# Compression rows streamed from whole pages over several queues, and routing in fewer, batched steps

## The reference

```python
def compress(raw, pe, w1, w2):
    n = S // CMP_BLOCK
    x = raw.reshape(B, n, CMP_BLOCK, 2, N_KV, HEAD_DIM) + jnp.transpose(pe, (1, 0, 2))[:, :, None, :]
    x = jnp.transpose(x, (0, 1, 3, 4, 2, 5)).reshape(B, n, 2, N_KV, CMP_BLOCK * HEAD_DIM)
    hdn = jax.nn.gelu(jnp.einsum('bnsgf,sfh->bnsgh', x, w1))
    return jnp.einsum('bnsgh,shd->bnsgd', hdn, w2)
```

## Time and profile before

| | us |
|---|---|
| median of 3 runs | 1498.45 |
| the three runs | 1494.69, 1498.45, 1502.95 |
| the profiled execution | 1498.93 |
| its span | 1496.8 |

### The profile page before, as it was taken

How to read it: one execution, slowest core, us unless ns; L and a number is a source line. 1 busy time by engine, 2 the same in 40 slices (tenths; PEclk the granted TensorE clock), 3 DMA queues, 4 the chain that set the end, 5 groups by cost and what they waited for, 6 DMA issues and landing times. The chain is left out here.

```text
span 1496.8 us, 21480 instructions
## 1 busy us (share of the span) xinstructions
PE 1282.4 (86%) x7890; PEld 929.3 (62%) x7891; DVE 742.0 (50%) x1547; ACT 528.9 (35%) x873; POOL 108.5 (7%) x159
## 2 busy tenths in 40 slices
PE   4289999999538989999997999279999999999962
PEld 1156666665326556656666887167788887788731
DVE  0012222221212545656676666768856658675248
ACT  0010000100000137755555221157646457665132
POOL 1000011000000000000000000001101001110040
PEclk9599999999757559999999999569999999999986
DMA  9753345500432063000003332559976769975572
GB/s 328 237 162 137 134 162 90 97 12 12 100 88 81 14 213 126 2 1 1 2 2 103 112 118 106 191 185 371 375 261 240 268 245 362 376 248 207 204 285 94
DMA packets 100626, 237.69 MB, mean 159 GB/s; under 512 B 19914, under 2 KB 27525, under 8 KB 100391
## 3 DMA queue, kind: packets, MB, share of 16 engines
q1 hardware_dynamic: 88951, 196.47, 39.3%
q0 software_dynamic: 8144, 27.62, 5.1%
q10 hardware_dynamic: 3456, 12.58, 2.1%
HBM read 198.61 MB, written 40.13 MB: 159 GB/s over the span
## 5 line engine op out<-in xcount | busy, mean ns | idle before, releaser
L2079 PE MATMUL psum<-w_hi,x_parts 128*128 128x512 f32 x736 | 240.3, 398 | 8.4 <-DVE x_parts L2198 7.5
L2191 DVE TENSOR_TENSOR w_lo<-raw,w_hi 128x2048 fp32r<-128x2048 f32 x96 | 215.6, 2288 | 56.8 <-ACT w_hi L2138 56.7
L2138 ACT CAST w_hi<-raw 128x2048 fp32r<-128x2048 f32 x96 | 178.5, 1912 | 93.5 <-DVE work L2209 50.6
L592 PE MATMUL psum<-low,high 128*128 128x512 f32 (+5 forms) x576 | 200.3, 502 | 0.0
L2079 PEld LDWEIGHTS psum<-w_hi,x_parts 128*128 128x128 f32 x736 | 139.9, 190 | 39.9 <-issue 11.0
L592 PEld LDWEIGHTS psum<-low,high 128*128 128x128 f32 (+1 forms) x576 | 105.4, 188 | 77.5 <-issue 66.9
L2079 PE MATMUL psum<-w_lo,x_parts 128*128 128x512 f32 x368 | 144.6, 393 | 0.0
L1501 DVE CUSTOM_DVE_ANT_0 low<-psum,high 128x512 f32<-128x512 f32 (+3 forms) x160 | 88.8, 593 | 78.1 <-PE psum L1341 77.8
L2079 PE MATMUL psum<-w_hi,a_parts 128*128 x368 | 121.2, 401 | 5.6 <-DVE a_parts L2204 5.5
L1469 ACT ACTIVATE low<-low,high 128x640 f32<-128x640 f32 (+7 forms) x128 | 93.0, 729 | 51.4 <-DVE high L1501 51.4
L1664 PE MATMUL psum<-wo_parts,mix_parts 128*128 128x512 f32 (+1 forms) x432 | 104.0, 398 | 6.8 <-DVE wo_parts L1801 6.2
(11 more groups left out here) (310 smaller groups left out, 1519.9 us busy)
## 6 DMA issues: line engine op xcount, KB each, us to landing
raw<-in_moe_w_gate SPq DMA_DIRECT2D x16, 2048.0 KB, 11.2
raw<-in_moe_w_up SPq DMA_DIRECT2D x16, 2048.0 KB, 12.0
raw<-in_moe_w_down SPq DMA_DIRECT2D x16, 2048.0 KB, 11.2
high<-in_w_mod SPq DMA_DIRECT2D x12, 2048.0 KB, 13.9
y_d<-work ACTq DMA_DIRECT2D x24, 512.0 KB, 7.0
high<-in_x_prompt SPq DMA_DIRECT2D x16, 512.0 KB, 3.9
y_d<-high SPq DMA_DIRECT2D x1, 8192.0 KB, 37.3
low<-in_w_in SPq DMA_DIRECT2D x3, 2048.0 KB, 15.1
```

Of the source, the lines that this page charges most:

```text
L592: mm = pe.matmul(c.bank(2 + n % 2)[0:T, 0:w], hT[i % 2][:, k, 0:T], c.w_in[:, k, a:a + w], start=(k == 0), stop=(k == KT - 1))
L2079: mm = pe.matmul(out, left[l][:, k * P:(k + 1) * P], w[:, bass.ds(at + k * step, 512)], start=n == 0, stop=n == len(steps) - 1)
L2138: act.copy(c.w_hi[:, at:at + PART // 2], c.raw[:, o:o + PART // 2]).then_inc(hi_done[p], 1)
L2191: dve.tensor_tensor(c.w_lo[:, at:at + PART // 2], c.raw[:, o:o + PART // 2], c.w_hi[:, at:at + PART // 2].bitcast(F32), ALU.subtract).then ...
```

## The change

In compression a piece becomes two whole rows: a partition holds a pair of rows as it lies in memory, 2 KB of it, so a prompt tile is one DMA and a page is one DMA into 64 partitions. There are eight buffers instead of three. SP asks for each sample's first page, GpSimd for its second; ScalarE asks for `w2` and `w1` at the block's start. Since the halves no longer land side by side, ScalarE copies each tile into one of two buffers `pairs`, in the order that the transposes want. `xcT` is written as [2][16][192], so that each product reads its 192 columns side by side.

In routing, independent steps lose their link; the constants come in two loads, the small one first; the count product comes first and alone, and the prefix over tiles is done by eight more products that add shifted counts in PSUM; the operands of these and of the slot products are 16-bit (0, 1, multiples of 128 and numbers under 128). The 36 comparisons become one over 594 elements, one over 2304, and two multiplications by 594; the token's number is carried in two parts, its row and its tile. The weights' sums move to the end of the block. Of `block_routing` only added lines are shown; those that they replace stand above.

```diff
@@ constants, memory_routing
-    cols = [strict, np.tile(NE - np.arange(NE), (P, 1)), np.tile(4 - np.arange(4), (P, 1)),
-            np.tile(MB * np.arange(1, 9), (P, 1)),
-            np.tile((np.arange(NE)[:, None] > np.arange(NE)[None, :]).reshape(1, -1), (P, 1)),
-            np.tile(np.arange(MAX_SLOTS + 1), (P, 1)), r[:, None] + P * np.arange(NT)[None, :], np.tile(r, (P, 1))]
+    cols = [np.tile(NE - np.arange(NE), (P, 1)), np.tile(4 - np.arange(4), (P, 1)),
+            np.tile(np.append(-1, MB * np.arange(1, 9)), (P, 1)), strict,
+            np.tile(MB * (np.arange(NE)[:, None] > np.arange(NE)[None, :]).reshape(1, -1), (P, 1)),
+            np.tile(r, (P, 1)), np.tile(P * np.arange(NT), (P, 1)), r[:, None]]
     c["cph4"] = np.concatenate(cols, 1)
     return {k: np.ascontiguousarray(v, np.float32) for k, v in c.items()}
...
-    c.scratch, = allocate(c, 0, ("scratch", 9216, F32))
+    c.scratch, c.scratch_16 = allocate(c, 0, ("scratch", 7168, F32), ("scratch_16", 4096, BF16))
...
@@ block_compression
-    xcT = c.view(W_, 4, NPAIR)
+    nblk = NC_P + NC_S * NB
+    xcT = c.view(W_, 2, CB // 2, 2 * nblk)
     w1 = c.view(W_ + 4 * NPAIR, 2, CB // 2, P)
     o = W_ + 4 * NPAIR + 2 * (CB // 2) * P
-    nat = [c.view(o + 512 * s, 4, 2, HD) for s in range(3)]
-    o += 3 * 512
+    NAT = 8
+    nat = [c.view(KVR_ + 1024 + 512 * s, 2, 4, HD) for s in range(NAT)]
...
+    def load_page(eng, n, pg):
+
+        if n >= NAT:
+            eng.wait_ge(paired, n - NAT + 1)
+        at = (n - 4) * NPAGE + pg
+        page = eng.value_load(c.page[0:1, at:at + 1], min_val=0, max_val=t["cache_cmp_kv"].shape[1] - 1)
+        src = t["cache_cmp_kv"][0, bass.ds(page, 1)].rearrange("n (p q) s g d -> p (n q s g d)", q=2)
+        dst = nat[n % NAT].rearrange("p q a d -> p (q a d)")
+        eng.dma_start(dst[64 * pg:64 * pg + 64, :], src).then_inc((nat_in, odd_in)[pg][n % NAT], 16)
 
     with nc.Block() as block:
+        @block.gpsimd
+        def _(pool):
+            for n in range(4, tiles):
+                load_page(pool, n, 1)
+
         @block.sync
         def _(sp):
             sp.dma_start(pe_n[0:32, :], t["cmp_pe"][0].rearrange("s (c q) d -> (s c) (q d)", q=2)).then_inc(pe_in, 16)
-            for n in range(tiles):
-                if n >= 3:
-                    sp.wait_ge(nt_ps, n - 2)
-                dst = nat[n % 3]
-                if n < 4:
-                    src = t["o_cmp_p"][0, 0, n * 256:(n + 1) * 256].rearrange("(p q) s g d -> p q (s g) d", q=2)
-                    for q in range(2):
-                        sp.dma_start(dst[:, :, q, :], src[:, q]).then_inc(nat_in[n % 3], 16)
-                else:
-                    b = n - 4
-                    for pg in range(NPAGE):
-                        at = b * NPAGE + pg
-                        page = sp.value_load(c.page[0:1, at:at + 1], min_val=0, max_val=t["cache_cmp_kv"].shape[1] - 1)
-                        src = t["cache_cmp_kv"][0, bass.ds(page, 1)].rearrange("n (p q) s g d -> p q (n s g) d", q=2)
-                        for q in range(2):
-                            sp.dma_start(dst[64 * pg:64 * pg + 64, :, q, :], src[:, q]).then_inc(nat_in[n % 3], 16)
-                if n == 3:
-                    sp.dma_start(w1, t["cmp_w1"][0].rearrange("s (c p) h -> p s c h", p=P)).then_inc(cw_in, 16)
-                    sp.dma_start(w2, t["cmp_w2"][0].rearrange("s h d -> h s d")).then_inc(cw_in, 16)
+            for n in range(4):
+                src = t["o_cmp_p"][0, 0, n * 256:(n + 1) * 256].rearrange("(p q) s g d -> p (q s g d)", q=2)
+                sp.dma_start(nat[n % NAT].rearrange("p q a d -> p (q a d)"), src).then_inc(nat_in[n % NAT], 16)
+            for n in range(4, tiles):
+                load_page(sp, n, 0)
...
-                pe.wait_ge(nat_in[n % 3], need[n])
+                pe.wait_ge(paired, n + 1)
-                                      nat[n % 3][:, sg, :, :].rearrange("p q d -> p (q d)"), c.ident)
+                                      pairs[n % 2][:, sg, :, :].rearrange("p q d -> p (q d)"), c.ident)
...
-                    cols = xcT[:, 2 * s:2 * s + 2, :].rearrange("p g (n c) -> p g n c", c=CB // 2)[:, :, :, k]
-                    mm = pe.matmul(c.bank(2 + s)[:, 0:2 * nblk].rearrange("p (g n) -> p g n", g=2), w1[:, s, k, :], cols,
+                    mm = pe.matmul(c.bank(2 + s)[:, 0:2 * nblk], w1[:, s, k, :], xcT[:, s, k, :],
...
+            act.dma_start(w2, t["cmp_w2"][0].rearrange("s h d -> h s d")).then_inc(cw_in, 16)
+            act.dma_start(w1, t["cmp_w1"][0].rearrange("s (c p) h -> p s c h", p=P)).then_inc(cw_in, 16)
+            for n in range(tiles):
+                act.wait_ge(nat_in[n % NAT], need[n])
+                if n >= 4:
+                    act.wait_ge(odd_in[n % NAT], need[n] - (16 if n >= NAT and n - NAT < 4 else 0))
+                if n >= 2:
+                    act.wait_ge(nt_ps, n - 1)
+                act.copy(pairs[n % 2], nat[n % NAT].rearrange("p q a d -> p a q d")).then_inc(paired, 1)
...
-                            xcT[:, 2 * s + g, n * P:(n + 1) * P].rearrange("p (n c) -> p n c", c=CB // 2),
-                            c.bank(n % 2)[:, (2 * s + g) * P:(2 * s + g + 1) * P].rearrange("p (n c) -> p n c", c=CB // 2),
-                            peT[:, s, :].unsqueeze(1).to_broadcast([P, 8, CB // 2]), ALU.add)
+                            xcT[:, s, :, g * nblk + 8 * n:g * nblk + 8 * n + 8],
+                            c.bank(n % 2)[:, (2 * s + g) * P:(2 * s + g + 1) * P].rearrange("p (n c) -> p c n", c=CB // 2),
+                            peT[:, s, :].unsqueeze(2).to_broadcast([P, CB // 2, 8]), ALU.add)
@@ block_routing
...
+            sp.dma_start(keys, t["cph4"][:, 0:rest]).then_inc(keys_in, 16)
+            sp.dma_start(consts, t["cph4"][:, rest:]).then_inc(consts_in, 16)
...
+            dve.tensor_tensor(m[:, 0:NP_TILES], oh1[:, 0:NP_TILES], oh2[:, 0:NP_TILES], ALU.add)
+            dve.tensor_tensor(m[0:NS, NP_TILES], oh1[0:NS, NP_TILES], oh2[0:NS, NP_TILES], ALU.add)
+            dve.wait_ge(consts_in, 16)
+            dve.tensor_copy(strict_h, strict).then_inc(cnt_ready, 1)
             dve.wait_ge(cnt_ps, 1)
...
+            linked(dve.tensor_reduce(totals, c.bank(1)[:, 0:NT * NE].rearrange("p (i e) -> p e i", i=NT), AX.X, ALU.add))
+            tt(over, over_last(totals, 9), limits.unsqueeze(1).to_broadcast([P, NE, 9]), ALU.is_gt)
             linked(dve.tensor_reduce(nb, over, AX.X, ALU.add))
...
             tt(tri, before, nb.unsqueeze(1).to_broadcast([P, NE, NE]), ALU.mult)
             linked(dve.tensor_reduce(starts, tri, AX.X, ALU.add))
...
+            dve.wait_ge(before_ps, 1)
+            tt(dest, c.bank(0)[:, 0:NT * NE].rearrange("p (i e) -> p i e", i=NT),
+               starts.unsqueeze(1).to_broadcast([P, NT, NE]), ALU.add)
+            tt(tmp.rearrange("p (k i) e -> p k (i e)", k=2), ohs.rearrange("p (k i) e -> p k (i e)", k=2),
+               dest.rearrange("p i e -> p (i e)").unsqueeze(1).to_broadcast([P, 2, NT * NE]), ALU.mult)
+            linked(dve.tensor_reduce(dests.rearrange("p i k -> p k i"), tmp.rearrange("p (k i) e -> p k i e", k=2), AX.X, ALU.add))
             linked(dve.tensor_copy(c.dest_i[:, :, :], dests))
 
             linked(dve.tensor_scalar(c.dest_y[:, :, :], c.dest_i[:, :, :], 7, None, ALU.arith_shift_right))
             linked(dve.tensor_copy(slot_f, c.dest_y[:, :, :]))
...
+            dve.scalar_tensor_tensor(out=place_f, in0=slot_f, scalar=-float(MB), in1=dests, op0=ALU.mult, op1=ALU.add)
+            n_slot = MAX_SLOTS + 1
+            tt(same_slot, slot_n.unsqueeze(1).to_broadcast([P, 2 * NT, n_slot]),
+               over_last(slot_f.rearrange("p i k -> p (i k)"), n_slot), ALU.is_equal)
+            dve.tensor_tensor(one_place, place_n.unsqueeze(1).to_broadcast([P, 2 * NT, P]),
+                              over_last(place_f.rearrange("p i k -> p (i k)"), P), ALU.is_equal)
+            dve.tensor_scalar(one_slot[:, :, 0, :], same_slot, row, None, ALU.mult)
+            dve.tensor_tensor(one_slot[:, :, 1, :].rearrange("p (i k) q -> p i k q", k=2),
+                              same_slot.rearrange("p (i k) q -> p i k q", k=2),
+                              tile_at.unsqueeze(2).unsqueeze(3).to_broadcast([P, NT, 2, n_slot]), ALU.mult).then_inc(dest_ready, 1)
+
+            linked(dve.tensor_scalar(slots[0:1], starts[0:1], 1.0 / MB, None, ALU.mult))
+            tt(table[0:1], slots[0:1].unsqueeze(1).to_broadcast([1, MAX_SLOTS, NE]), over_last(slot_n[0:1, 0:MAX_SLOTS], NE), ALU.is_le)
             linked(dve.tensor_reduce(exps[0:1], table[0:1], AX.X, ALU.add))
             linked(dve.tensor_scalar(exps[0:1], exps[0:1], -1.0, None, ALU.add))
...
+            dve.tensor_copy(c.slot_e[:, :], exps[0:1])
+            dve.tensor_copy(ends[0:1, 0:NE], slots[0:1])
+            tt(ends[0:1, NE:NE + 1], slots[0:1, NE - 1:NE], nb[0:1, NE - 1:NE], ALU.add)
             dve.tensor_copy(c.start_e[:, :], ends[0:1]).then_inc(tab_ready, 1)
```

(21 more changed lines are left out.)

111 lines of the change are left out of this document (44 added, 67 removed).

## The result

The changed kernel takes 1450.39 us (median of 4 runs, 1447.23 to 1451.47) beside 1499.91 us for the kernel before in the same series; the ratio is 0.967, 95% interval 0.964 to 0.970. The forecast was 1451 us. That it lands so close is partly luck: by the profiles the page loads gave 21.1 us and not 28, routing gave 13.5 and not 11, and a stretch that the forecast had left alone came out 6.6 us shorter.

The account below looks back on a forecast made before the run. The prediction took compression to be bound by page issue and slow strided products, and routing by one VectorE chain. 1498.93 - 28 - 8 - 11 = 1451.9 us, 1451 at the median; range 1440 to 1463.

Parts of the forecast that it names:

- three parts: Compression's page loads, compression's products with `w1`, and the routing block, with gains of 28, 8 and 11 us.
- last wanted byte: Compression loads: 16.0 us of transfer plus 4 for `state_win`, ending at 417.5 +-4; products begin at 419.
- Bounds of the kernel before: Compression: pages bound by issue on SP, 32 DMAs 1.08 us apart, DMA engines only 0.31 busy.
- Issue of the pages: Compression: eight pages each, SP 1.10 us apart, done near 407.2; GpSimd 1.3 us each, done near 406.5.
- Rival 1: Compression loads: transfers at 184 GB/s take the gain back, products at 428, total 1461 us; chance 0.12.
- Rival 2: Page loads: the split brings nothing, 16 x 1.10 us hides under transfers, also 1451 us; shares 0.55 with the forecast.
- ScalarE's copy and VectorE's adds: Compression: 0.6 us per copy, adds 0.88 up to 1.3 us a tile, both hidden except the last tile's copy.
- Products: Compression's 64 records with `w1`: contiguous columns cut 21.1 us to 13.3; gain 8 us (0 to 10).
- What is late next: Next block's `cph2` and `state_win`: landed near 421, TensorE comes near 436, covered by 15 us.
- Routing: Routing block: shorter waits, fewer comparisons and 16-bit products end it at 971.6, not 983.02; gain 11 us (9 to 13).
- The sum: Whole kernel: 1498.93 - 28 - 8 - 11 = 1451.9 us, 1451 at the median of runs.

Follow-up runs that it names:

- one_queue: The changed kernel with all 16 pages asked for by SP and none by GpSimd; 1454.24 us, ratio 0.971 to the kernel before.
- w1_ahead_one: w1_ahead with all 16 pages asked for by SP; 1447.70 us, ratio 0.969 to the kernel before.
- w1_third: The changed kernel with ScalarE asking for `w1` after its copy of tile 3, not at the block's start; 1449.31 us, ratio 0.970 to the kernel before.
- w1_ahead: The changed kernel with `w1` loaded by SP in the projection block before, `xcT` in other columns; 1439.06 us, ratio 0.962 to the kernel before.
- half_w1: The changed kernel with only the keys' half of `w1` loaded and used for values too, so results differ; 1460.81 us.
- sums_early: The changed kernel with the expert weights' sums put back ahead of the wait for the counts; 1451.51 us, ratio 0.969 to the kernel before.
- routing_only: The kernel before with only the new routing block, its compression unchanged; 1476.66 us, ratio 0.987 to the kernel before.

## Why the prediction was right, and where it was not

In short: which waits would go, and why, was right in all three parts. Wrong was the step "last wanted byte", that is, how fast the transfers run and what they wait for once issue no longer holds them. Each step in its order:

**Bounds of the kernel before: right.** 16 page DMAs on SP take 19.02 us for the same bytes (one_queue, w1_ahead_one), where the 32 of before started from 408.8 to 442.3 us; they are 1.19 us each beside the 1.10 of the earlier trace rows. The pieces grew in the same edit, and no run takes the two apart; for issue speak the engines' share of 0.31 before and, in w1_ahead_one, of 0.36 to 0.40 from 400 to 415 us.

**Issue of the pages: right in its prices.** GpSimd's interval was taken as 1.3 us and is 1.15; the instruction 0.52 us against 0.55. SP's was taken as 1.10 and is 1.15 (8 pages in 9.21 us, w1_third) to 1.19. What was wrong is that they run through: SP ended at 411.8, GpSimd at 412.3, not near 407, since both waited for buffers.

**Last wanted byte: wrong.** The step said 16.0 us of transfer by the rates 292 and 368 GB/s, 4 us for `state_win`, and products at 419, that is 23.35 us after the block's start, with bounds up to 424. Measured 30.01, or 425.7 on that axis: past the bound. The gain was 21.1 us, not 28. The 6.7 us divide by w1_third: its last byte comes at 24.5 us, with all engines busy, at 240 to 277 GB/s in its first four windows of 5 us. Against the forecast's 417.5 - 395.65 = 21.9 that is 2.6 us, the rate. The mix is not all of it: tiles and pages ran at 261 GB/s without `w1` too (w1_ahead), so the 368 GB/s of the expert weights was the wrong row for them, though their pieces are 2 KB as well. Why they are slower, no run shows. In the changed kernel `w1` lands at 420.9 - 393.6 = 27.3, another 2.8 us, the order: beside `w1`, prompt tiles 2 and 3 land 11.2 and 14.6 us after their request and not 4.8 and 5.4 as in w1_third, and they hold the buffers of the last pages. The tail behind is 2.7 us, not 1.5, another 1.2. (This splits one profile of each kernel; the load of kernels without an edit spreads over 2.3 us.) I had counted bytes and queues, and not which bytes release a buffer. Eight buffers for twelve tiles looked ample.

**Rivals 1 and 2.** Rival 1 (a mix at 184 GB/s, products at 428) named the right quantity: the mix gave 219 to 249 GB/s while `w1` was under way, between that row and the ones I took. (The 184 itself was no full rate: the engines' share in that row is 0.80. And the trace books `w1` and `w2` in 1312 packets for 2.16 MB, 1.6 KB each, so the 512-byte pieces that this rival counted on are not what was moved.) With `w1` in front the second queue saved nothing (28.0 to 30.3 against 27.75 us), without it 9.2 us. By the rule that the prediction cites from the Trainium skill, "DMA: Bandwidth & Descriptors", section "Issuing engines are not separate DMA queues", several issuing engines save only issue time. These runs agree with that, but the time saved was not small: 16 page DMAs of one engine are 19.02 of 27.45 us in w1_ahead_one. Rival 2 holds in its result, but not by its reason. One queue is not hidden under a shorter transfer; it is a bound of its own at 27.5 us, as near as the other by accident. By its own figures, 416 + 2.3 and a page's tail of 2.6, it should have been 420.9 and not the forecast's 419.

**ScalarE's copy and VectorE's adds: right.** 0.62 us a copy against 0.6. An add takes 0.22 us as before, so nothing was paid for the jumps.

**Products: right, with two small errors that cancel.** 13.38 us against 13.3. The record is faster at full clock than forecast (0.163 against 0.175 us), but the clock rose only after 17 records instead of 14. Where it was up from the first record, they took 10.67 (w1_ahead, half_w1).

**What is late next: right.** `state_win`, the last of the loads for the next block, landed at 428.1 (asked for at 412.95, 15.1 us), TensorE came at 440.6.

**Routing: gain 13.5 us, not 11.** Up to the first count product 1.9 us were saved against 1.4 forecast, at the wait for counts 1.7 against 1.3; counts to slot matrices take 8.53 us against 8.7; the tail 4.3 us instead of 5.4. The mis-sized term is the 18 products: 3.0 was taken from bounds of 2.0 and 4.0, and they take 1.29 us, under the lower bound. That bound gave a 16-bit record of 66 columns a quarter of the time of the two float32 records that it replaces; it takes a sixth. The ids now wait for VectorE's table work beside the products, 2.1 us.

**Attention: 6.6 us that the forecast has not.** By the profiles they go with TensorE's clock: in the windows from 70, 80 and 90 us after the next block's first product, it was 0.50, 0.50, 0.84 in the kernel before and 0.81, 1.00, 1.00 in the changed one (the number ahead of the share):

```profile
541.50:551.50 10.00, 10.00 (x48) 6.39 (x47) 2.41 (x16) 5.23 (x24) 0.61 (x1) 0.50 1.04 224
551.50:561.50 10.00, 10.00 (x44) 5.82 (x43) 4.70 (x21) 5.29 (x21) 0.61 (x1) 0.50 1.02 395
561.50:571.50 10.00, 10.00 (x74) 6.33 (x70) 6.00 (x27) 6.79 (x23) 0.61 (x1) 0.84 1.03 421
```
```profile
510.60:520.60 10.00, 9.77 (x64) 6.32 (x64) 4.29 (x23) 6.73 (x31) 0.61 (x1) 0.81 1.05 215
520.60:530.60 10.00, 9.70 (x74) 6.24 (x74) 7.85 (x38) 7.99 (x30) 0.61 (x1) 1.00 1.02 398
530.60:540.60 10.00, 10.00 (x82) 5.69 (x80) 5.21 (x22) 8.15 (x29) 0.86 (x2) 1.00 1.03 423
```

Counted from that product, the clock rises some 20 us earlier, and more records pass in each window. It is not the effect of one edit: of the ten profiles with the new compression five have the early value (468.6) and five the late one (475 to 478), one_queue, sums_early and w1_third among these. Both profiles with the old compression are late, but that does not make it theirs. routing_only's profile is its execution of 1483.74 us; of its six, two take 1483.7 and 1484.2 us at a mean granted clock of 0.900 and 0.899, and four take 1475.6 to 1476.7 us at 0.908 to 0.911. In the first series the kernel before is split too: 1490 to 1496 us at 0.901 to 0.905, 1498 to 1506 at 0.894 to 0.898. So it looks as if one and the same kernel does both; only the profiled executions can be split by stretch, so this is not shown. What the rise hangs on stays open, since no run was made for it. If those four of routing_only were early, that would also explain why its total is better than its block. The medians differ by 49.5 us, of which compression (28.8) and routing (13.5) are 42.3; the other 7 I cannot divide between chance and change. The changed kernel's profile is the fastest of its four executions, so its early value need not be the typical one.

**The sum.** -28 was 21.1, -8 was 7.7, -11 was 13.5: 42.3 instead of 47. That is 5 us short. The time had them all the same, from stretches that the forecast had left alone: this is luck.

## What to carry to other kernels

When loads stop being bound by their issue, list what each buffer waits for, not only the bytes: a large transfer that is needed last and asked for first delays the small ones that release buffers. Put it behind them (load 30.0 to 24.6 us here), or better into a stretch whose DMA engines are idle (18.3 us). A split over two queues can be worth nothing and 9 us in the same kernel, by what else is in the way; test it again after the next bound is gone.

## What the runs showed of the hardware

- Three queues together (`w1`, prompt tiles and pages) moved 219 to 249 GB/s with all DMA engines busy; without `w1`, tiles and pages moved 261 (w1_ahead); as the last of them landed and `state_win` took over, 341 (420 to 425 us).
- `w1` (2 MB) landed 26.6 us after its issue where it was asked for first beside SP's and GpSimd's queues, 18.5 us with GpSimd's queue unused (one_queue), 17.2 us where it was asked for behind the prompt's tiles (w1_third).
- A register-addressed page DMA, with its register load, costs GpSimd 1.15 us and SP 1.15 to 1.2: the same.
- At half clock a 16-bit product of 66 columns passes in 0.07 us, a float32 record of 33 columns in 0.22.
- A float32 record of 192 columns that reads 64 bytes apart takes 0.324 us at either clock; contiguous, it halves when the clock doubles (0.320 to 0.163).
- In ten profiles with the new compression TensorE's granted clock rose to full and stayed there some 74 to 76 us after the next block's first product in five, and 93 to 97 us after it in the other five; the stretch to routing is 7 to 10 us longer in the latter.
